# Mixing blocks: attention scores one product group later on TensorE, with the query copies and the biased scores one group later on ScalarE and VectorE

## The reference, cut to what matters

```python
z = h @ w_in                                   # h is 256 x 2048
q, k, v, u, ga, gc = split(z)                  # q, k, v: 16 heads of 128
scores = q @ k.T * scale - slope * distance    # per head, causal, 256 keys
o = softmax(scores) @ v
y_attn = o @ w_attn_out
y_conv = conformer_conv(u)                     # depthwise convolution of 31 taps, norm, projection
out = (sigmoid(ga) * y_attn + sigmoid(gc) * y_conv) @ w_out
```

## Time and profile before

| | |
|---|---|
| median of three runs | 2110.32 us (2107.88 to 2113.97) |
| the profiled execution | 2110.9 us, its span from first to last instruction 2109.1 us |
| PE busy | 2091.4 us, 99% of the span |
| VectorE busy | 1902.9 us, 90% |
| ScalarE busy | 1417.5 us, 67% |
| GpSimd busy | 221.9 us, 11% |
| DMA | 562.95 MB, 267 GB/s in the mean |
| mean granted TensorE clock | 0.998 of full speed |

### The profile page before, as it was taken

One profiled execution on the slowest core, in us unless ns is written; L12 is line 12 of the kernel. 1 busy time (PEld: TensorE's weight loads), 2 busy tenths in 40 slices (PEclk: granted clock), 3 DMA queues, 4 the chain that ended last, 5 costly groups with the idle time before them and its releaser, 6 DMA issues.

```text
span 2109.1 us, 23576 instructions
## 1 busy us (share of the span) xinstructions
PE 2091.4 (99%) x9362; PEld 1730.0 (82%) x9362; DVE 1902.9 (90%) x1422; ACT 1417.5 (67%) x1315; POOL 221.9 (11%) x351
## 2 busy tenths in 40 slices
PE   9999999999999999999999999999999999999998
PEld 7888888888888888888888888878888888888886
DVE  8899999999997889999999986899899999999996
ACT  6677777778775546766676435555677777778773
POOL 0111111110110000111100000000111111101110
PEclk9999999999999999999999999999999999999999
DMA  9788998899896759988898556885798899899892
GB/s 372 253 293 263 277 271 268 287 304 275 290 276 235 274 156 309 299 260 273 305 301 258 212 195 237 297 264 200 245 293 265 273 276 267 287 299 280 287 285 112
DMA packets 90958, 562.95 MB, mean 267 GB/s; under 512 B 12896, under 2 KB 13280, under 8 KB 30944
## 3 DMA queue, kind: packets, MB, share of 16 engines
q1 hardware_dynamic: 66240, 437.69, 54.7%
q0 software_dynamic: 24608, 123.75, 27.3%
HBM read 540.42 MB, written 20.97 MB: 266 GB/s over the span
## 4 chain that ended last, share of the span: by engine, by line
PE 88%; DVE 8%; DMA 2%; ACT 1%; issue 1%; SPq 0%; DVEq 0%; ACTq 0%
PE acc L2463 15%; PE acc L2465 15%; PE acc L2464 15%; PE tb L2463 12%; PE tb L2465 12%; PE tb L2464 12%; DVE g_lo L1446 3%; DVE cacc L1921 3%; DMA g_raw<-in_groups 2%; PE acc L2410 1%; PE acc L2412 1%; PE acc L2411 1%; PE tb L2449 1%; DVE w_lo L1423 1%; DVE g_raw L1454 1%; PE acc L2517 1%
## 5 line engine op out<-in xcount | busy, mean ns | idle before, releaser
L1446 DVE TENSOR_TENSOR g_lo<-g_raw,g_hi 128x2048 fp32r<-128x2048 f32 x528 | 1197.3, 2286 | 125.1 <-ACT g_hi L874 124.6
L874 ACT ACTIVATE g_hi<-g_raw 128x2048 fp32r<-128x2048 f32 x528 | 1005.7, 1915 | 330.5 <-DVE g_raw L1454 127.3
L2463 PE MATMUL acc<-g_hi,xF_hi 128*128 128x512 f32 x1216 | 476.9, 392 | 1.7 <-DVE g_lo L1446 1.1
L2465 PE MATMUL acc<-g_hi,xF_lo 128*128 128x512 f32 x1216 | 473.6, 389 | 0.0
L2464 PE MATMUL acc<-g_lo,xF_hi 128*128 128x512 f32 x1216 | 473.2, 389 | 0.0
L2463 PE MATMUL tb<-g_hi,xF_hi 128*128 128x512 f32 x760 | 296.2, 390 | 0.0
L2465 PE MATMUL tb<-g_hi,xF_lo 128*128 128x512 f32 x760 | 295.7, 389 | 0.0
L2464 PE MATMUL tb<-g_lo,xF_hi 128*128 128x512 f32 x760 | 295.6, 389 | 0.0
L1454 DVE TENSOR_TENSOR g_raw<-g_raw,g_raw 128x2048 f32<-128x2048 f32 x122 | 278.8, 2285 | 1.5
L2463 PEld LDWEIGHTS acc<-g_hi,xF_hi 128*128 128x128 f32 x1216 | 228.4, 188 | 49.7 <-issue 2.1
L2465 PEld LDWEIGHTS acc<-g_hi,xF_lo 128*128 128x128 f32 x1216 | 228.2, 188 | 48.0
(11 more groups left out here) (194 smaller groups left out, 2146.3 us busy)
## 6 DMA issues: line engine op xcount, KB each, us to landing
g_raw<-in_groups SPq DMA_DIRECT2D x372, 1024.0 KB, 7.3
g_raw<-in_groups POOLq DMA_DIRECT2D x86, 1024.0 KB, 8.5
raw<-in_stream SPq DMA_DIRECT2D x48, 512.0 KB, 4.4
bounce<-h_sq POOLq DMA_DIRECT2D x40, 256.0 KB, 5.2
h_in<-bounce POOLq DMA_DIRECT2D x160, 64.0 KB, 2.7
ln_gb<-in_ln SPq DMA_DIRECT2D x6, 1024.0 KB, 7.2
g_raw<-in_groups SPq DMA_DIRECT2D x6, 512.0 KB, 9.5
res<-in_x_rows SPq DMA_DIRECT2D x1, 2048.0 KB, 15.8
```

Of the source, the lines that this page charges most:

```text
L874: act.activation(g_hi[:, n % RING], source[:], ACT.Copy).then_inc(g_hi_ready, 1)
L1446: dve.tensor_tensor(g_lo[:, n % RING], source[:], f32(g_hi[:, n % RING]), ALU.subtract).then_inc(g_lo_ready, 1)
L2463: pe.matmul(bank, x_hi_ap, g_hi[:, n % RING, blk], start=begin, stop=False, skip_group_check=True)
L2465: return pe.matmul(bank, x_lo_ap, g_hi[:, n % RING, blk], start=False, stop=end, skip_group_check=True)
```

## The change

Nothing is added or left out; on three engines instructions change places in the blocks with heads (1 to 4).

- ScalarE: the high half of P3a is made before the query copies, not after.
- VectorE: the low half of P6b is made before the first biased scores, that of P3b before the second ones and the maxima.
- PE: the scores of pair 0 come behind P5b, not P5a; those of pair 1 behind P3a, not P6a. `wait_fork(f, g, 1)` goes with P3a.

```diff
@@ ScalarE, mixing_block @@
                 split_sum(f, g, "P6a", "qa", "T2a")
+                split_loaded(f, g, "P3a", "ua")
                 if heads:
                     queries_turned(g - 1)
-                split_loaded(f, g, "P3a", "ua")
                 split_sum(f, g, "P6b", "qb", "T2b")
@@ VectorE, mixing_block @@
                 lo_group(f, g, "P3a", "ua")
+                lo_group(f, g, "P6b", "qb")
                 if heads:
                     biased_scores(g - 1, 0)
-                lo_group(f, g, "P6b", "qb")
+                lo_group(f, g, "P3b", "ub")
                 if heads:
                     biased_scores(g - 1, 1)
                     maxima(g - 1)
-                lo_group(f, g, "P3b", "ub")
                 taps(counts[2])
@@ TensorE, mixing_block @@
                 product_group(f, g, "P5a", W, S1, 0, begin=True)
+                product_group(f, g, "P5b", W, S1, 1)
                 if heads:
                     scores(g - 1, 0)
-                product_group(f, g, "P5b", W, S1, 1)
                 wait_fork(f, g, 0)
                 product_group(f, g, "P6a", X, S2, 0)
+                wait_fork(f, g, 1)
+                product_group(f, g, "P3a", Z, S4, 0)
                 if heads:
                     scores(g - 1, 1)
-                wait_fork(f, g, 1)
-                product_group(f, g, "P3a", Z, S4, 0)
                 product_group(f, g, "P6b", X, S2, 1)
```

## The result

The changed kernel takes 2114.94 us (median of 20 runs, 2113.94 to 2116.12), the kernel before 2110.76 us (20 runs). The ratio is 1.002, with a 95% interval from 1.0014 to 1.0026: 4.2 us more, 0.2%, which is within the 0.3% that I called no change, and it lies 0.6 us above the forecast of 2114.3 us.

The account below looks back on a forecast made before the run. PE's own order was taken as the bound, so only PE's waits count: -2.4 - 0.2 + 6.4 + 0.2 = +4.0 us, giving a 2114.3 us median. Forecast's own range 2111 to 2117.5 us; 8 in 10 for 2109 to 2119.

Parts of the forecast that it names:

- First pair: PE, blocks 1 and 2: P5b covers the 1.34 and 1.09 us waits before the first scores, both go: -2.4 us.
- Transpose in block 2: PE's 0.2 us wait at a softmax-weight transpose goes, as the last gate group's load starts several us earlier: -0.2 us.
- Second pair: P7a on PE, blocks 1 to 4: 8.44 us chain against 6.83 us cover, so 1.61 us wait each: +6.4 us.
- The chain keeps its length: VectorE, block 1: P3b's low half ends at 857.1, before the second pair's first head at 858.8; VectorE still waits.
- What is late next: turn_p(0), the first transpose of weights: needed 13.6 us after the second pair, comes at 13.9; no second wait, but near.
- Restart: PE's first matmul behind a wait is some 0.1 us longer; two go, four come: +0.2 us, bounds 0 and 0.5.
- The two small terms: The block 2 transpose's wait going, -0.2 us, and the longer first matmuls behind PE's waits, +0.2 us.
- the first: P7a: its cover is larger than 1.1 us, so no wait comes back; -2.6 us alone, 2107.7 us; chance 0.07.
- The second, P7b's accumulating load: P7b's high half waits for POOL's load, P7a loses the full 2.72 us per block: +8.3 us, 2118.6 us; chance 0.07.
- The third: TensorE's clock falls to the 1.2 GHz level behind P7a's new waits: +13.2 us, 2123.5 us; chance 0.02.

Follow-up runs that it names:

- the second profile: The kernel before, profiled once more with nothing changed, to see how much its waits at the first pair of scores move from run to run: 2110.87 us.

## Why the prediction was right, point by point

- **First pair, -2.4 us.** Right: no wait is left in any block. The size is that of one profile; the second profile has 2.2 us, all of it in block 2. Moved without the second pair, it showed less in the time (0.6, 1.1 and 1.9 us), since PE was then held up elsewhere in blocks 1 and 2.
- **Transpose in block 2, -0.2 us.** Right: no wait at a transpose in the changed kernel. By the starts the wait had been 0.3 us.
- **Second pair, +6.4 us.** Right in mechanism and size. Chain 8.44 us, cover 6.83 us, wait 1.61 us, in four blocks alike. The runs that separate the parts bear it out: the second pair alone keeps the wait to the digit, and putting it back takes the wait away. Cutting the chain on ScalarE takes it away too, with the pair left where the change put it. One product group more of delay makes the wait longer by just that group.
- **The chain keeps its length.** Right: VectorE waited for the scores (2.38 us) with P3b's low half done.
- **What is late next.** Right: turn_p(0) had no wait. In block 1 it starts at 872.50, and four scalings from 871.11 on end at about 872.07: 0.4 us to spare where I had 0.3. That it was near shows where the copy goes ahead of the exponents: 1.0 us at the longest came back there. P4a's low half was covered.
- **Restart, +0.2 us.** From P7a to the first transpose are 5.62 us where two groups take 5.44: 0.18 us a restart, where I took 0.1. What the other terms leave of the 4.18 us is 0.5 us, the upper bound that I gave.
- **The sum.** +4.0 forecast, +4.18 between block 1's P5a and block 4's Q4. The two small terms were off by 0.1 and 0.3 us in opposite directions; that the sum came out closer than they did is luck. Of the 0.64 us between forecast and measured time 0.44 lie in the kernel before, 2110.32 us in the three runs that I had and 2110.76 us in twenty.

Of the rivals, the first fell, since four waits came. The second, P7b's accumulating load, decided nothing in the changed kernel, where ScalarE waited for no load of weights from 840 to 1110 us; but the runs on the first pair and on the copy's place showed the mechanism in one block each, at 0.9 us and about 0.6 us. I had taken its 8.0 to 22.2 us from all the accumulating loads; P7b's own, the second of four in each block, took 13.1 to 14.7 us in the kernel before, well short of the 17 us from which it would have cost. The third was no matter at 1.6 us. The run with one more group showed that it is real: there the clock did fall, and I had left it out of the theory's number for that run. The Trainium skill (TensorE: Matmul & The Clock Gate, HAM oscillation) says that gaps in front of groups of matmuls can put the clock back to its lower level; behind the 4.3 us waits the trace agrees (0.50 to 0.61 in the windows above), and behind the 1.6 us waits of this change the granted clock stayed at 1.00. The example there is of waits of some 3 to 5 us, so it bears on the former, and the 2123.5 us that the prediction drew from it for waits of 1.6 us did not follow.

Why does the version that keeps the second pair's old place gain 2 us and not the whole 2.6? The starts tell: from P5a of block 1 to Q4 of block 4 it takes 245.90 us, 2.12 us less than before. Blocks 1 and 2 take 67.19 and 67.02 us from P5a to P5a where block 3 takes 66.73; PE loses 0.1 to 0.2 us at a time there, at the second transposes, the outputs and P7a, too little each to stand in the list of waits. Not settled: what makes the queries' way out up to 2.4 us shorter or longer in one program, and what it is in ScalarE's move that makes P7b's load late.

## What to carry to other kernels

Moving an instruction behind more work hides the wait in front of it and takes the same work away from whatever hangs on its result: before moving it, follow its consumers on every engine to the next place where the bounding engine waits, and compare that chain with the cover that is left. Here 1.1 us of cover stood against one group of 2.72 us. Move each instruction by itself where that can be done: of two moves of scores in one change the first, with what goes with it on ScalarE and VectorE, was worth about 2 us (0.2 to 4.0), and the second cost 6.

## What the runs showed of the hardware that I had not expected

- Waits of 4.3 us between runs of matmuls brought PE's granted clock from 1.00 down to 0.50 for a while, in each of four blocks, at 1.9 us a time in the mean; waits of 1.6 us did not.
- One program's transfers moved by 2.5 us between two profiles (845.93 and 848.43 for the same copies), and the time moved by nothing, because what one block gained the next one lost: from P5a of block 1 to Q4 of block 4 are 248.02 and 248.07 us.
- P7b's accumulating load took 15.8 to 16.3 us from issue to landing in block 2 in the three runs with P3a's high half made earlier and the second pair at its old place, and 13.4 to 14.4 us in three profiles without that move.
- A wait behind a matmul is written about 0.15 us shorter than the starts give it (1.45 and 1.61 us).
